# Down projection as seven half-size products, with row and weight sums made in the gate/up stage and kept in DRAM

## The reference, cut to what matters

```python
# x is (1, 1024, 1024); D_FF = 2816
f = rms_norm(x, pre_ffn_g[i])
f = (jax.nn.silu(f @ w_ffn_gate[i]) * (f @ w_ffn_up[i])) @ w_ffn_down[i]
x = x + rms_norm(f, post_ffn_g[i])

e = p[i] @ w_ple_up[i]                      # p is (1024, 256)
gate = jax.nn.sigmoid(x @ w_ple_gate[i])
x = x + rms_norm(gate * e, ple_norm_g[i])
```

## Time and profile before

| | before |
|---|---|
| median of 3 runs | 1583.91 us |
| profiled execution, device time | 1583.49 us |
| its span (first to last instruction) | 1581.6 us |
| PE busy | 1493.2 us (94%) |
| DVE busy | 1009.8 us (64%) |
| ACT busy | 574.1 us (36%) |
| DMA queue, share of 16 engines | 26.8% |
| gate/up, tiles 2 to 21 (830.4 to 1211.0 us) | 380.6 us |
| down (1211.0 to 1453.3 us) | 242.3 us |
| last stage, to the end of the span | 128.3 us |

### The profile page before, as it was taken

The page is one execution under the profiler, slowest core; times in us unless marked ns, Lnnn a source line. Parts: engine busy times, 40 slices in busy tenths (PEclk is TensorE's granted clock), DMA queues, the critical chain, the costliest instruction groups (busy, mean ns, idle before and its releaser), DMA issues.

```text
span 1581.6 us, 19303 instructions
## 1 busy us (share of the span) xinstructions
PE 1493.2 (94%) x7192; PEld 1190.7 (75%) x7192; DVE 1009.8 (64%) x1450; ACT 574.1 (36%) x1065; POOL 244.4 (15%) x368
## 2 busy tenths in 40 slices
PE   5999999998789989999999999999999999999997
PEld 5887788876656556766688888888888887887886
DVE  4648978997578899982486556655564433444553
ACT  5344443215434434533452222322222334333221
POOL 5444456517600000000000000000000000000000
PEclk9999999999899999999999999999999999999999
DMA  6212233326010000001122222222224434553110
GB/s 199 68 51 76 75 91 105 138 75 253 14 54 27 28 27 28 28 14 41 41 80 74 86 80 80 80 93 81 80 80 152 167 140 152 181 205 148 53 67 40
DMA packets 105241, 140.41 MB, mean 89 GB/s; under 512 B 8896, under 2 KB 72128, under 8 KB 105152
## 3 DMA queue, kind: packets, MB, share of 16 engines
q1 hardware_dynamic: 105152, 139.22, 26.8%
HBM read 108.79 MB, written 30.41 MB: 88 GB/s over the span
## 4 chain that ended last, share of the span: by engine, by line
PE 72%; DVE 10%; DVEq 6%; issue 5%; POOL 3%; ACT 3%; DMA 1%; SPq 1%; POOLq 0%; ACTq 0%
PE ps L601 20%; PE ps L603 20%; PE ps L602 20%; PE ps L827 4%; DVEq L1603 4%; DVE m L1600 3%; DVE lm L1692 2%; DVE sc L1589 2%; DVEq L1601 2%; PE ps L772 1%; PE ps L789 1%; PE ps L780 1%; ACT pt L1212 1%; PE ps L718 1%; PE ps L716 1%
## 5 line engine op out<-in xcount | busy, mean ns | idle before, releaser
L1600 DVE MAX8 m<-sc 128x8 f32<-128x384 f32 (+5 forms) x192 | 171.1, 891 | 13.1 <-issue 2.9
L1602 DVE MATCH_REPLACE8 sc<-m,sc 128x384 f32<-128x384 f32 (+5 forms) x192 | 168.2, 876 | 0.3 <-issue 0.3
L601 PE MATMUL ps<-dh,hth 128*128 128x512 f32 x352 | 137.1, 390 | 2.2 <-ACT fo L1408 1.9
L602 PE MATMUL ps<-dl,hth 128*128 128x512 f32 x352 | 136.9, 389 | 0.0
L603 PE MATMUL ps<-dh,htl 128*128 128x512 f32 x352 | 136.9, 389 | 0.0
L2060 POOL TENSOR_TENSOR smf<-smf,sml 128x1 f32<-128x1 f32 x16 | 8.7, 550 | 774.5 <-DVE smf L1991 671.4
L601 PE MATMUL ps<-wbh,xth 128*128 128x512 f32 (+1 forms) x320 | 120.1, 375 | 2.5 <-DVE xtl L1496 2.5
L602 PE MATMUL ps<-wbl,xth 128*128 128x512 f32 (+1 forms) x320 | 119.0, 372 | 0.0
L603 PE MATMUL ps<-wbh,xtl 128*128 128x512 f32 (+1 forms) x320 | 119.0, 372 | 0.0
L1928 DVE TENSOR_TENSOR dl<-dr,dh 128x512 fp32r<-128x512 f32 x44 | 30.4, 692 | 123.8 <-ACT dh L1389 123.8
L1203 ACT ACTIVATE lm<-lm,sml 128x128 f32<-128x128 f32 (+7 forms) x64 | 49.6, 774 | 127.1 <-DVE sml L1692 126.5
(11 more groups left out here) (267 smaller groups left out, 3559.7 us busy)
## 6 DMA issues: line engine op xcount, KB each, us to landing
hr<-hidden_rows SPq DMA_DIRECT2D x44, 512.0 KB, 4.1
raw<-in_w_in SPq DMA_DIRECT2D x48, 256.0 KB, 3.0
dr<-in_w_ffn_down SPq DMA_DIRECT2D x44, 256.0 KB, 2.7
raws<-in_w_ffn_gate SPq DMA_DIRECT2D x21, 512.0 KB, 4.0
raws<-in_w_ffn_up SPq DMA_DIRECT2D x21, 512.0 KB, 5.3
ret_rows<-stg SPq DMA_DIRECT2D x32, 320.0 KB, 3.4
rp<-ret_rows SPq DMA_DIRECT2D x8, 1280.0 KB, 7.4
hidden_rows<-hb SPq DMA_DIRECT2D x20, 512.0 KB, 2.8
```

Of the source, the lines that this page charges most:

```text
L601: pe.matmul(o, ah, wh, start=start, stop=False, skip_group_check=resumes)
L602: pe.matmul(o, ah, wl, start=False, stop=False, skip_group_check=resumes)
L1600: v.max(M8[:, :], sc_b)
L1602: v.match_replace(sc_b, M8[:, :], sc_b, PICKED)
```

## The change

The down projection takes the same seven-product scheme. Hidden tiles are computed in another order (`tile_of`: 0, 11, 1, 12, ...), so that tiles phi and phi + 11 are finished one after the other. For each of 11 pairs DVE makes four row sums (`row_sums`, from the two hidden tiles) and four weight sums (`down_sums`, from four blocks of the down weights that SP loads for it), and SP stores them in DRAM (`hidden_sums`, `down_sums`), two stores of 512 KB and four of 256 KB. The down stage is then 77 steps (`DOWN` times 11) of four `mm3`; each loads 256 KB of rows and 256 KB of weights into a ring of six. Products accumulate in banks 0 to 3 and 4 to 7. Between products ACT (`read_product`) and DVE (`read_sum`) take them out into `FO`. Rows 512 to 1023 (`ROWS_IN_TURN`) are finished first and enter the last stage first; the transposes of the first two blocks stand between the last down steps. `s1b` and `u2b` have one buffer in place of two. `store_down_sums(phi)` and `store_row_sums(phi)` wait on SP for DVE's sums.

```diff
@@ hidden tiles, their order, and what is stored when
-    def weights_landed(g):
-        return 32 * ((g + 1) // 2)
+    def tile_of(g):
+        return g // 2 + FH * (g % 2)
...
+    ROW_SUMS_AT = {2 * phi + 2: phi for phi in range(1, FH - 1)}
+    WT_ORDER = tuple(range(FH - 2)) + (FH - 1, FH - 2)
+    WT_AT = dict(zip(list(range(3, 2 * FH - 2, 2)) + [2 * FH - 2, 2 * FH - 1], WT_ORDER))
+    DOWN = (1, 6, 2, 7, 5, 4, 3)
+    DSTEPS = len(DOWN) * FH
+    DRING = 6
@@ SP
+        def store_row_sums(phi):
+            sp.wait_ge(s["v_hs"], 4 * (phi + 1))
+            sp.wait_ge(st_h[phi % 2], hidden_stored(phi))
+            for j in range(2):
+                sp.dma_start(hs_dram[phi, j], HB[phi % 2][j]).then_inc(st_h[phi % 2], 16)
+        def load_down_blocks(phi):
+            before = WT_ORDER.index(phi)
+            sp.wait_ge(s["move_wt"], 128 * before)
...
+            for b, (f, dh) in ((12, (phi, 1)), (11, (phi, 0)), (22, (phi + FH, 1)), (21, (phi + FH, 0))):
+                sp.dma_start(WT[b][:, :], w_ffn_down[0, f * P:(f + 1) * P, dh * 512:(dh + 1) * 512])\
+                  .then_inc(s["move_wt"], 16)
+        def store_down_sums(phi):
+            sp.wait_ge(s["v_wt"], 4 * (WT_ORDER.index(phi) + 1))
+            for i, b in enumerate((11, 12, 22, 21)):
+                sp.dma_start(wt_dram[phi, i], WT[b][:, :]).then_inc(s["move_wt"], 16)
...
         for g in range(G0, FT):
             if g > G0:
                 store_hidden(g - 1)
+            if g == G0:
+                store_row_sums(0)
+            if g in WT_AT:
+                load_down_blocks(WT_AT[g])
+            if g in ROW_SUMS_AT:
+                store_row_sums(ROW_SUMS_AT[g])
+            if g in WT_AT and g + 2 < FT:
+                store_down_sums(WT_AT[g])
             if g + 2 < FT:
                 sp.wait_ge(s["t_gu"], gu_at(g, 4))
                 gate_up(g + 2)
             if g == FT - 2:
+                store_down_sums(WT_AT[g])
                 down(0)
-        for n in range(1, 3):
+        for n in range(1, 4):
             down(n)
+        store_down_sums(WT_AT[FT - 1])
         store_hidden(FT - 1)
...
+        for n in range(4, DRING):
+            down(n)
+        store_row_sums(FH - 1)
+        row_gain(GPF2, post_ffn_g, "load_gain")
+        row_gain(GPL, ple_norm_g, "load_gain")
+        sp.wait_ge(s["move_wt"], wt_stored(FH - 2))
...
+        for n in range(DRING, DSTEPS):
+            down(n)
@@ PE
+        def down(n):
+            m, phi = DOWN[n // FH], n % FH
+            i, opens, ends = n % DRING, m in (1, 6, 5), phi == FH - 1
             pe.wait_ge(s["v_dhl"], 2 * (n + 1))
+            for r in (0, 2, 1, 3) if n == 0 else range(4):
+                if phi == 0:
+                    down_bank_free(m, r)
+                rs = slice(r * P, (r + 1) * P)
+                ins = mm3(bank(DOWN_BANK[m] + r), AH[i][:, rs], AL[i][:, rs], BH[i][:, :], BL[i][:, :],
+                          phi == 0 and opens, ends, not opens)
...
+        for n in range(DSTEPS):
+            down(n)
+            if n in (DSTEPS - 3, DSTEPS - 2):
+                x2_transposes(n - (DSTEPS - 3))
@@ DVE
+        def row_sums(phi):
...
+            v.tensor_tensor(o[1][:, 1, :], a[0][:, 1, :], a[1][:, 1, :], ALU.add).then_inc(s["v_hs"], 1)
+            dve.wait_ge(s["v_hs"], 4 * phi + 1)
...  (three more, each after the one before)
+        def down_sums(phi):
+            dve.wait_ge(s["move_wt"], wt_landed(phi))
+            base_ = 4 * WT_ORDER.index(phi)
+            for i, (o, a, b) in enumerate(((11, 12, 11), (12, 22, 12), (22, 22, 11), (21, 21, 22))):
+                if i:
+                    dve.wait_ge(s["v_wt"], base_ + i)
+                v.tensor_tensor(WT[o][:, :], WT[a][:, :], WT[b][:, :], ALU.subtract).then_inc(s["v_wt"], 1)
+        row_sums(0)
...
             row_half("c22", g)
             if g + 1 < FT:
                 weights_lo(g + 1, 1)
                 weights_lo(g + 1, 2)
             else:
-                down_lo(1)
+                for n in range(2, 4):
+                    down_lo(n)
+            if g in ROW_SUMS_AT:
+                row_sums(ROW_SUMS_AT[g])
+            if g in WT_AT:
+                down_sums(WT_AT[g])
             row_half("c21", g)
             row_half("h1", g)
...
+        for n in range(4, DSTEPS):
+            down_lo(n)
+            if n == 5:
+                row_sums(FH - 1)
```

More of the change, by code:

```diff
@@ L216, in build @@
     WG = sb("wg", [P, KT, 2, D], 76, F32R)
[L217 removed]
+    WGR = sb("wgr", [P, KT, 2, D], 76)
+    WUR = sb("wur", [P, 2, D], 156)
     WUH = sb("wuh", [P, 2, D], 148, F32R)
@@ L544, in down @@
[L544 to L551, removed]
+            elif n < DRING:
+                sp.wait_ge(s["t_gu"], GU_ALL)
+            else:
+                sp.wait_ge(s["t_dn"], dn_at(n - DRING))
@@ L552, in _ @@
+            if kind == "w":
+                src = w_ffn_down[0, (phi + i) * P:(phi + i + 1) * P, dh * 512:(dh + 1) * 512]
+            else:
+                src = wt_dram[phi, i]
+            sp.dma_start(RWB[n % DRING][:, :], src).then_inc(load_dr[n % DRING], 16)
+        for g in range(2):
+            store_hidden(g)
         for g in range(G0, FT):
@@ L951, in _ @@
                 product(g, m)
[L954 to L958, removed]
-            pe.wait_ge(s["v_dhl"], 2 * (n + 1))
[L961 to L979, removed]
-            else:
-                m.then_inc(s["t_dn"], 1)
@@ L1430, in _, with square_half, read_product @@
-        for n in range(3, 2 * FT):
+        def square_half(dh, r):
+            if dh == 0 and r < 4:
+                act.wait_ge(s["a_fo"], 4 + r + 1)
+            elif dh == 0:
+                act.wait_ge(s["v_fo"], 12 + (r - 4) + 1)
+            elif r < 4:
+                act.wait_ge(s["v_fo"], 16 + r + 1)
+            else:
+                act.wait_ge(s["v_fo"], 8 + (r - 4) + 1)
+            square_into((f"fo{dh}", r), FO[:, dh, r, :], 2 * r + dh)
+        def read_product(m, r):
+            act.wait_ge(s["t_dn"], acc_at(m, r))
+            if m == 1:
+                act.wait_ge(st_h[0], sums_stored(FH - 1))
+            sc.copy(FO[:, 0, 4 + r if m == 1 else r, :], bank(r)).then_inc(s["a_fo"], 1)
@@ L1475, in _ @@
+        for i in range(RT):
+            act.wait_ge(s["t_gt"], i + 1)
+            if i >= 1:
+                act.wait_ge(s["v_u"], i)
+            else:
+                act.wait_ge(s["t_dn"], dn_at(DSTEPS - 1))
+            sc.activation(SGG[:, :], pair(0), ACT.Sigmoid).then_inc(s["a_sig"], 1)
+            if i + 2 < RT:
+                x2_hi(i + 2)
+            act.wait_ge(s["v_u"], i + 1)
+            square_into(("u", i), UU[i % 2][:, :], 32 + ROWS_IN_TURN[i])
     @block.vector
@@ L1944, in _ @@
             else:
-                down_lo(0)
+                for n in range(2):
+                    down_lo(n)
             row_half("u3", g)
```

583 lines of the change are left out of this document (316 added, 267 removed).

## The result

| | before | after |
|---|---|---|
| median | 1582.82 us (4 runs, 1581.54 to 1585.44) | 1656.19 us (4 runs, 1651.64 to 1656.54) |
| ratio to before, 95% interval | | 1.0455 [1.0431, 1.0478] |
| profiled execution, span | 1583.49, 1581.6 us | 1656.54, 1654.7 us |
| gate/up | 380.6 us | 477.0 us |
| down | 242.3 us | 225.4 us |

The change makes the kernel 4.5% slower. The forecast was 1622 us with a range up to 1652: the direction was right, and 34.3 us are missing. The three stages give +96.4 - 16.9 - 4.2, and what lies ahead of gate/up -2.2, in sum +73.1 us of span.

A forecast was written before the change was run, and what follows sets the result against it. PE's matmuls were taken to bound gate/up and down, so new PE waits add in full. -30.0 + 52.7 + 0.7 + 14.8 + 2.0 - 1.8 = +38.4 on 1583.5 gave 1621.9 us, range 1588 to 1652.

The forecast's parts named there:

- Removed matmuls: Down stage: 924 matmuls in place of 1056, at 0.227 us each, -30.0 us.
- The waits of the loop: Gate/up, 17 tiles: raws loads behind the sums' stores delay u2, so PE waits 3.1 us each, +52.7 us.
- First tile: Start of gate/up: the first row sums on DVE delay u2 of tile 2, +0.7 us.
- Start of down: Tile 21 and first down steps: loads behind stores make PE wait, 8.5 us at step 6; +14.8 us, bounds 5 and 22.
- The clock: Down: the 8.5 us wait loses the full clock once, +2.0 us; no fall counted for the loop's 3.1 us waits.
- Entry of the last stage: Between down and last stage: PE's 2.20 us wait for x2 shrinks to about 0.4, -1.8 us.
- Issue order only: Rival, gate/up: the stores' data do not hold the loads, 26.8 us for 52.7, so 1596 us; chance 0.22.
- The sums are hidden: Rival, gate/up: u2 stays inside its 1.36 us slack, so PE does not wait; 1555 us, chance 0.09.
- The sums' place on DVE: Rival, gate/up: DVE's work as a bound of its own, 13.9 of 19.0 us a tile; counted at nothing.
- this rival: Gate/up: each of 17 waits is followed by matmuls at 1.2 GHz, +34 us, 1656 us; chance 0.2.

The follow-up runs named there:

- experiment 5: Changed kernel with SP issuing raws loads ahead of the sums' stores, down's first steps asked for earlier, last row sums and last-stage inputs later: 1553.67 us, 0.9816 of before.
- experiment 2: Changed kernel plus twelve matmuls into an unused bank ahead of product 7 on tiles 4 to 20: 1632.51 us, 1.0328 of before.
- Experiment 1: Changed kernel, but on tiles 3 to 19 SP issues the raws loads before waiting for and storing the sums: 1571.86 us, 0.9937 of before.
- experiment 4: Changed kernel, but each store of sums writes 32 of 512 columns and down reads a hidden tile and down weights instead of sums: 1624.18 us, 1.0271 of before.
- Experiments 5 and 6: The second of the two: changed kernel with only the reordered loads and stores at the start of down, loop order untouched: 1637.28 us, 1.0341 of before.
- experiments 3 and 4: The first of the two: changed kernel plus four matmuls into an unused bank ahead of product 7 on tiles 4 to 20: 1657.15 us, 1.0488 of before.

## Why the prediction was wrong

The stages of experiment 5 are a kernel without these waits at full clock, so the loss can be parted by their rows. Gate/up of the kernel after is 477.0 - 382.5 = 94.5 us longer: 59.5 us of idle time against 0.5, and 417.5 us of busy time against 382.0 for the same matmuls. Down is 12.2 us longer: 11.3 us idle against 1.6, and 2.5 us more of busy time.

Not all of the 35.5 us is slow clock. The 30 matmuls behind each of the 18 waits took 33.3 us longer in sum than at 0.227 us each, and behind a wait after which the clock stays the same count is 0.12 to 0.17 us. So about 31 us is the clock, 28.8 of it behind the 17 waits for u2, which is what experiment 2 gave back. The rest comes with each wait at any clock.

- **Removed matmuls, -30.0.** Right: down is -29.1 us in experiment 5, its matmuls 0.227 us apart.
- **The waits of the loop, +52.7.** Right in mechanism and place, and near in size: 17 waits, tiles 4 to 20, for u2, behind landings at +15.5 to +16.3. PE's rows give 3.25 us each, 55.2 in sum. My 3.1 was counted from start to start; so counted, and with the 0.13 us behind each, the waits cost 60 us, 7 more than forecast. Experiment 1 shows the cause, experiment 4 that its parts were 2.19 and 1.06.
- **First tile, +0.7.** It cost 0.4: product 7 of tile 2 ends 11.27 us after the first matmul of the stage, where it was 10.88.
- **Start of down, +14.8.** 4.3 us for product 4 of tile 21 (2.3 predicted), nothing for bank 3 (1.0), 10.06 us for step 6 (8.5), and 1.3 us more in a second wait (3.0): 15.6. Experiments 5 and 6 take most of it away by SP's order, for 18.2 to 18.9 us in all. That this is more than the waits fits the clock behind them (2.2 us behind that for u3, up to 2.5 in down), which was not parted by a run.
- **The clock, +2.0: this step failed.** It read "for waits of 3.1 us the rows leave it open; the forecast has none". In place of none the runs showed a fall behind every one of the 17 waits, 28.8 us, and behind that for u3, 2.2 us. The fall that I had expected, behind the long wait of down, cost at most 2.5. So the term should have been some 33 us instead of 2.0, which is most of the 1656.2 - 1621.9 = 34.3 us that are missing; the 7 us from the length of the waits are in part offset by smaller terms, among them 2.2 us ahead of gate/up and 2.4 in the last stage that I did not forecast. The mechanism was among the rivals, priced at +34 and 1656 us, with a chance of 0.2; that this meets the measured 1656.2 so closely is luck, since its price was 5 us too high and the waits 7 too low. The two rows that I had were an idle time of 3.62 us with a fall and one of 2.20 without, and the 2.9 us of idle time that I expected lie midway. They gave no reason for a term of nothing, nor for so low a chance.
- **Entry of the last stage, -1.8.** Right in direction: the wait of 2.20 us is gone, 0.3 is left. The stage is 4.2 us shorter, since 16 transposes now stand inside down as well.
- **The rivals.** "Issue order only" falls with experiment 4, where the data cost 18.0 us of waits. "The sums are hidden" was false for this kernel, but its 1555 us is what the same arithmetic takes once the queue is reordered (1553.67). The sums' place on DVE is no bound: DVE works 275 of 382.5 us in experiment 5.

The Trainium skill, "TensorE: Matmul & The Clock Gate", section "Why this matters for your kernels", which tells to keep gaps between bursts short, spoke for this rival, and experiment 2 agrees: filled gaps kept the clock at 1.00. It allows gaps as long as some of those of experiments 3 and 4 behind which the clock fell, from 1.98 us on; there the measurement decides.

Gate/up of experiment 5 is still 1.9 us longer than before (382.5 against 380.6). Of this 0.4 is the first tile, and 1.2 lies in three tiles where the raws landed at +12.3 to +12.7 (before at +12.0 at the latest) and u2 was ready after the +16.3 at which product 7 is due. Why they land later there, and why some idle times between 2.0 and 2.7 us lose the clock and some do not (below), stays open.

## What to carry to other kernels

On a queue that runs in order, a store that waits for a computation puts that wait in front of every load behind it: ask for the loads first, and give the store what is left. Here that order was worth 84 us and the arithmetic 30. Price a repeated wait of the matrix engine as its length plus the slow clock behind it, here 3.3 + 1.7 us; if the gap is bounded by something else, matmuls into an unused bank win the second part back. And read busy time beside the granted clock: 35 us of the loss stood in the rows as work, 31 of them slow clock.

## What the runs showed of the hardware

- The price of a fall: in gate/up of the kernel after and experiments 1 to 6 the 30 matmuls behind an idle time that lost the clock took 1.4 to 3.0 us longer than at 0.227 us each. Behind the 40 such idle times from 1.98 to 3.2 us it was 1.5 to 1.8 us; behind the 22 from 3.2 to 4.31 us it was 2.3 to 3.0 ten times and 1.4 to 1.8 twelve times.
- Over the idle times of PE from 0.24 us on in gate/up of the kernel after and experiments 1 to 6: up to 1.88 us none of 27 lost the clock; of 26 between 1.98 and 2.72 us 20 did; from 2.79 us on all 42 did.
- SP's issue of one load is not a constant: `raws` of the up weights took 1.42 and 0.89 us behind the stores of two successive tiles, and 1.11 and 0.58 us ahead of them in experiment 1. In the kernel before, without such stores, it was 0.58 us on most tiles and 0.79 to 1.33 us on every third.
